# Odd layer: decode value units in 52 slots instead of 58, and the output projection's operand made in pairs inside the last block

## The reference

```python
q, kc, vc, ks, vs, kw, vw, g, z = split(rms_norm(h) @ w_in_c)
# compressed branch: scores against block sums, o_cmp, importance of blocks
# selected branch: the top 16 blocks per K/V head, o_sel; window branch: o_win
o = gate[:, :, 0] * o_cmp + gate[:, :, 1] * o_sel + gate[:, :, 2] * o_win
y = (o * silu(z)) @ w_out_c
h = h + y
h = h + sigmoid(h @ w_ple_gate) * (p @ w_ple)
```

## Time and profile before

| | us |
|---|---|
| runs (3) | 1796.89, 1798.23, 1798.7 |
| profiled execution, its time | 1798.01 |
| its span, first to last instruction | 1796.3 |
| PE busy | 1727.9 (96%) |
| PE weight loads | 1592.9 (89%) |
| DVE busy | 1094.8 (61%) |
| ACT busy | 816.1 (45%) |
| CZ blocks, first matmul to last value matmul | 1343.06 to 1574.78 |
| first matmul of OUT1 | 1581.09 |

### The profile page before, as it was taken

One profiled execution on the slowest core, in us unless ns is written; L12 is line 12 of the kernel. 1 busy time (PEld: TensorE's weight loads), 2 busy tenths in 40 slices (PEclk: granted clock), 3 DMA queues, 4 the chain that ended last, 5 costly groups with the idle time before them and its releaser, 6 DMA issues.

```text
span 1796.3 us, 43681 instructions
## 1 busy us (share of the span) xinstructions
PE 1727.9 (96%) x17501; PEld 1592.9 (89%) x17501; DVE 1094.8 (61%) x1900; ACT 816.1 (45%) x1703; POOL 188.0 (10%) x360
## 2 busy tenths in 40 slices
PE   6999999988999989999998999999999999989998
PEld 5899999888888879999988988888888888889998
DVE  4478888777644445354458998754555544454554
ACT  4344444444334324345466444433345545544554
POOL 3000000000000000000000003333332443300000
PEclk9999999999999979999999999999999999989999
DMA  7888888653587738669765557787787888764464
GB/s 239 312 276 275 276 273 280 228 152 118 175 271 263 250 106 310 225 227 298 241 197 178 153 149 224 251 268 230 233 248 224 280 255 260 252 235 148 153 188 131
DMA packets 287097, 406.49 MB, mean 226 GB/s; under 512 B 18641, under 2 KB 223088, under 8 KB 285881
## 3 DMA queue, kind: packets, MB, share of 16 engines
q1 hardware_dynamic: 260196, 320.00, 55.4%
q0 software_dynamic: 26624, 83.92, 14.7%
q10 hardware_dynamic: 92, 0.02, 0.0%
HBM read 391.43 MB, written 12.45 MB: 225 GB/s over the span
## 4 chain that ended last, share of the span: by engine, by line
PE 80%; DVE 14%; ACT 2%; issue 2%; DMA 1%; SPq 0%; ACTq 0%; DVEq 0%
PE PJ L1819 50%; PE XB L2232 4%; PE XB L1845 4%; DVE w_low L1138 3%; PE XB L2244 2%; PE XB L2320 2%; PE XB L2110 2%; PE XB L2301 2%; PE XB L1959 1%; DVE scr L1157 1%; PE XB L2276 1%; DVE proj L1157 1%; PE XB L1862 1%; PE XB L1919 1%; PE XB L1998 1%
## 5 line engine op out<-in xcount | busy, mean ns | idle before, releaser
L1819 PE MATMUL PJ<-xh,w_up 128*128 128x264 f32 x3072 | 924.6, 301 | 25.0 <-DVE xl L1181 10.7
L1819 PE MATMUL PJ<-xl,w_up 128*128 128x264 f32 x3072 | 876.8, 285 | 0.0
L1819 PE MATMUL PJ<-xh,w_low 128*128 128x264 f32 x3072 | 875.7, 285 | 0.0
L1138 DVE TENSOR_TENSOR w_low<-wring,w_up 128x512 fp32r<-128x512 f32 x768 | 524.7, 690 | 409.3 <-ACT w_up L678 399.1
L678 ACT CAST w_up<-wring 128x512 fp32r<-128x512 f32 x768 | 473.7, 618 | 414.8 <-PE PJ L1819 396.9
L1819 PEld LDWEIGHTS PJ<-xh,w_up 128*128 128x128 f32 x3072 | 583.5, 190 | 49.8 <-DVE w_low L1138 16.5
L1819 PEld LDWEIGHTS PJ<-xl,w_up 128*128 128x128 f32 x3072 | 583.1, 190 | 3.1
L1819 PEld LDWEIGHTS PJ<-xh,w_low 128*128 128x128 f32 x3072 | 581.0, 189 | 0.0
L646 POOL DMA_DIRECT2D cring<-in_cache_c_sel_kv_dram x256 | 137.3, 537 | 1332.3 <-issue 1035.0
L955 ACT COPY kcmp<-XB 128x512 f32<-128x512 f32 x80 | 46.8, 585 | 149.9 <-PE XB L2232 149.8
L1488 DVE COPY kcmp<-XB 128x512 f32<-128x512 f32 x80 | 55.3, 691 | 74.3 <-PE XB L2232 73.1
(11 more groups left out here) (330 smaller groups left out, 1503.1 us busy)
## 6 DMA issues: line engine op xcount, KB each, us to landing
wring<-in_w_in_ab_dram SPq DMA_DIRECT2D x144, 512.0 KB, 4.6
cring<-in_cache_c_cmp_kv_dram SPq DMA_DIRECT2D x128, 512.0 KB, 5.4
cring<-in_cache_c_sel_kv_dram POOLq DMA_DIRECT2D x256, 256.0 KB, 3.9
wring<-in_w_in_c_dram SPq DMA_DIRECT2D x112, 512.0 KB, 4.6
wring<-in_w_ple_gate_dram SPq DMA_DIRECT2D x64, 512.0 KB, 4.2
cring<-in_cache_a_kv_dram SPq DMA_DIRECT2D x48, 512.0 KB, 5.2
wring<-in_w_out_ab_dram SPq DMA_DIRECT2D x32, 512.0 KB, 4.4
cring<-in_cache_c_win_kv_dram POOLq DMA_DIRECT2D x64, 256.0 KB, 4.6
```

What stands on the lines that cost most here:

```text
L1138: nc.vector.tensor_tensor(w_low[:, e % NE], raw(e), w_up[:, e % NE].bitcast(F32), ALU.subtract).then_inc(sem("w_lo"), 1)
L1819: ins = nc.tensor.matmul(PJ[(2 * bl + c) % 4][:, 0:T], w[:, e % NE, k, tileT(c)], x[:, kx, :], start=(kx == 0 and w is w_up and x is xh), ...
```

## The change

The table `VU` now puts the 160 value units into slots 5 to 56 instead of 5 to 62: samples 0, 2, 4 and 6 take six slots (3, 3, 3, 3, 4, 4 units), the others seven. The operand of OUT1 is made in eight pairs of chunks instead of four groups of four. Pairs 0 to 6 are made inside the last CZ block by two new tables, `CAT1_MUL` (slot of the product on DVE) and `CAT1_UP` (slot of the cast on ACT and the subtraction on DVE); pair 7, which needs the last prompt output, is made in the first two slots of OUT1. A cast waits until PE has left the slot that reads the old `xh` pair.

```diff
-            parts = (3, 3, 3, 3, 2, 2, 2, 2) if b_ in (2, 5) else (3, 3, 3, 3, 3, 3, 2)
+            parts = (3, 3, 3, 3, 3, 3, 2) if b_ % 2 else (3, 3, 3, 3, 4, 4)
...
-        assert t_ == 63
+        assert t_ == 57
+        CAT1_MUL = {58: (0, 1, 2), 59: (3, 4), 60: (5,), 61: (6,)}
+        CAT1_UP = {59: (0, 1), 60: (2, 3), 61: (4,), 62: (5,), 63: (6,)}
...
+            def out_up(p):
+                last = CZ + 7
+                a = slice(2 * p, 2 * p + 2)
+                act.wait_ge(sem("x_tmp"), 8 * CAT1 + p + 1)
+                if p < SLOTS - 1:
+                    act.wait_ge(sem("w_used"), 7 + 7 * last + p + 1)
+                else:
+                    act.wait_ge(sem("proj_made"), 4 + 2 * last + 2)
+                nc.scalar.copy(xh[:, a, :], cat[:, a, :]).then_inc(sem("x_hi"), 1)
...
+                for p in CAT1_UP.get(t, ()):
+                    out_up(p)
             for x in CU[8 * SLOTS - 1]:
                 pc_out(x // 2)
             z_rows(7)
-            upper_x(CAT1, cat)
             for t in range(8 * SLOTS):
                 m, s = t // SLOTS, t % SLOTS
                 upper(OUT1 + m, s)
+                if t == 1:
+                    out_up(7)
...
+            def out_pair(p):
+                a = slice(2 * p, 2 * p + 2)
+                if p == 0:
+                    dve.wait_ge(sem("OT_taken"), 2 + B)
+                dve.wait_ge(sem("cu_o_taken"), 4 * p + 4)
+                dve.wait_ge(sem("z_silu"), 8 + 2 * p + 2)
+                nc.vector.tensor_tensor(cat[:, a, :], cat[:, a, :], proj[:, a, :], ALU.mult).then_inc(sem("x_tmp"), 1)
+            def out_low(p):
+                a = slice(2 * p, 2 * p + 2)
+                dve.wait_ge(sem("x_hi"), 8 * CAT1 + p + 1)
+                nc.vector.tensor_tensor(xl[:, a, :], cat[:, a, :], xh[:, a, :].bitcast(F32), ALU.subtract).then_inc(sem("x_lo"), 1)
...
+                for p in CAT1_MUL.get(t, ()):
+                    out_pair(p)
+                for p in CAT1_UP.get(t, ()):
+                    out_low(p)
...
-            add_new(B - 1)
-            dve.wait_ge(sem("cu_o_taken"), 32)
-            dve.wait_ge(sem("OT_taken"), 2 + B)
-            dve.wait_ge(sem("z_silu"), 8 + 16)
-            for n in range(4):
-                a = slice(4 * n, 4 * n + 4)
-                nc.vector.tensor_tensor(cat[:, a, :], cat[:, a, :], proj[:, a, :], ALU.mult).then_inc(sem("x_tmp"), 2)
-                if n >= 1:
-                    lower_x(CAT1, cat, n - 1)
-            lower_x(CAT1, cat, 3)
             dve.wait_ge(sem("resid_in"), 32)
             for m in range(8):
                 for s in range(SLOTS):
                     lower(OUT1 + m, s)
+                    if (m, s) == (0, 0):
+                        out_pair(7)
+                    elif (m, s) == (0, 1):
+                        out_low(7)
```

## The result

The changed kernel takes **1804.86 us** (median of six runs, 1803.09 to 1807.53), where the kernel before takes 1798.47 beside it (1793.29 to 1799.53): a ratio of 1.0042, 95% interval 1.0027 to 1.0058. By the medians it is slower by 6.4 us (the ratio makes it some 7.6), where the forecast, 1800.4, had said no difference that could be told; the median lies just past the end of its range, 1804.8. The profiled execution took 1803.59 us with a span of 1801.7 (before 1798.01 and 1796.3).

What follows compares the result with a forecast made beforehand. The z projection was taken as bound by PE's own work, the boundary hole behind it worth 9.1 us. Terms -1.1 + 0 + 2.5 + 1.0 = +2.4 us on 1798.01 gave 1800.4 us, range 1795.0 to 1804.8.

Steps and rivals of the forecast that it cites:

- Term 4: Value units packed into 52 slots instead of 58: +1.0 us, one of four six-slot samples losing time; range 0 to 4.4.
- the units come late: Rival: PE waits at the ring in all four six-slot samples, term 4 is 4 instead of 1; 1803.4 us, chance 0.25.
- Term 3: Slots 58 to 63: new DVE and ACT steps delay PE, +2.5 us; DVE chain alone 1.9, range 0.8 to 4.4.
- Term 1: Boundary to OUT1: PE runs three slots, then idles 5.2 us instead of 6.31 awaiting the copy-back; -1.1 us.
- term 2: Clock behind the boundary hole: falls as before with the same loss, 0 us; bounds -2.8 to +2.3.
- The rivals on the faster side: At the boundary: copy-back is no bound, 1792.4 us, chance 0.05; or clock stays up, 1797.6 us, chance 0.18.
- What a later wait gives: Boundary: waiting later for the copy-back, ahead of which eight splits do not read its data, would give 1792.4 us.

Runs made afterwards that it cites:

- experiment 3: The changed kernel with the selected value pages read from fixed page numbers instead of the page table's: 1797.37 us, 0.9995 of the kernel before.
- experiment 2: The changed kernel with DVE's wait for the copy-back moved from OUT1's first split to the first addition to the hidden state: 1796.49 us.
- 9: The changed kernel with both fixed value page numbers and DVE's copy-back wait moved to the first addition to the hidden state: 1792.42 us.
- experiment 1: The kernel before with only the change's table of value units, OUT1's operand still made between the blocks: 1800.94 us.
- 5: The changed kernel with roles swapped, odd samples taking six slots and even ones seven: 1803.62 us.
- 8: The changed kernel with odd samples in six slots and DVE's copy-back wait ahead of the first addition to the hidden state: 1797.70 us.
- experiment 6: The changed kernel with 20 more small transfers on GpSimd's queue at the program's start: 1845.02 us.

## Why the prediction was wrong

- **Term 4, the units, failed: +1.0 forecast, +7.2 in the trace.** The medians give 6.4 (the changed kernel against experiment 3), 3.5 (experiment 2 against 9) and 3.5 (experiment 1, with the 0.8 of its last slots), each to within 2 to 3.5 us: the size is not settled, but all three are above 1.0. The step that failed set the queue's 20.7 us for a sample against a sample's 22.3 us. That is a mean over 20 units of two prices. The 16 pages come first, and 17.4 us of queue meet 14.7 us of PE. The ring had to lend 2.7 us in three of the four six-slot samples, and a pause or a late landing (6.35 us where the median is 4.2) was then enough. The upper end, 4.4 us, was too low as well: it counted 1.1 us in each of four samples, and the trace has one wait of 2.5 us with a fall of the clock, 3.2 us, which the term did not hold.
- The rival "the units come late" is what took place in kind, and was named with 0.25. It had PE waiting in all four six-slot samples, and its time, 1803.4, came near by luck: the trace has one long wait, in a seven-slot sample, with the clock behind it. Its own "306 of 318 GB/s" was the wrong reason: with fixed pages the same bytes came in time.
- **Term 3, the last slots, was right in size, +2.5 forecast, 2.5 measured, and in part by luck.** The sum had PE wait for the probabilities of unit 31 in slot 62. PE does not wait there. It waits in slots 59 and 61 for ACT's copies and in slot 60 for DVE's score step. DVE's new steps delay the scores and two of the new casts stand ahead of the copies of slot 61, so DVE and ACT were the right engines. Experiment 1 divides it: 1.8 for the pairs, near the 1.9 of the DVE chain, and 0.8 because no unit covers a wait that was there anyway. DVE's new steps in slots 58 to 63 are 14, not 13; the sum does not use the number. PE's waits in these slots:

```profile
PE XB L2329 <- ACT scr L1057: 1.7, 2, 1.1
...
PE XB L2320 <- DVE small L1686: 0.9, 1, 0.9
```

- **Term 1, the boundary, was right in mechanism: -1.1 forecast; with term 2 the boundary measured -2.0.** Three slots, the hole and its releaser came as said; the hole was 5.54 us, 0.8 shorter than before, not 5.2: the copy-back took 8.66 us, not 8.5, and from the landing (1591.16) to PE's start it was 0.86, not 0.73.
- **Term 2, the clock, was forecast at 0 and gave back about 1.0 us.** The low stretch was 6.8 us, not 10.2, with 3.58 us of matmuls in it: 1.8 us lost where 2.80 were lost before.
- The rivals on the faster side did not come: the copy-back was a bound, and the clock fell. What a later wait gives was put at 1792.4; with the units and the last slots as they are it is 1796.49, without the units' loss 1792.42.

## What to carry to other kernels

Compare a queue with its reader over the stretch in which the dear transfers come, not over a whole round that also holds cheap ones: a ring of buffers lends its depth once, and the next round may find it empty. A wait belongs ahead of the first instruction that reads the data: here, placed earlier, it held the weight splits behind it in DVE's queue. And where PE runs dense, a wait of a few microseconds may cost its own length and a fall of the clock besides, here 2.5 us and 3.2 more.

## What the runs showed of the hardware

- **The clock fell inside dense work behind one wait.** PE is busy for 195.63 of the 202.60 us around it (97%); a wait of 2.5 us (2.6 and 3.3 in experiments 1 and 2) brought 0.50 for 6.8 us. Waits of 1.7 and 1.9 us in experiments 5 and 8 did not, one of 1.6 in experiment 6 did, for 3.4 us. So no single length of wait divides them here.
- **A pause of 2.3 to 2.4 us in GpSimd's queue** stands ahead of the same unit in all eleven traces, the kernel before included, where that unit still had time in hand (it landed 4.8 us ahead of its use). Twenty transfers more did not move it, nor did the fixed pages, which take address loads out ahead of it. Its cause is open.
